# The narrow experts of a mixture-of-experts layer: plain float32 products in two column halves in place of split float32r products

## What is computed

```python
def swiglu(x, w_gate, w_up, w_down):
    return (jax.nn.silu(x @ w_gate) * (x @ w_up)) @ w_down

def moe_swiglu(x, router_w, router_b, w_gate, w_up, w_down):
    ...
    top_logit, top_e = lax.top_k(logits, TOP_K)
    gate = jax.nn.softmax(top_logit, axis=-1)
    ...
    # rows of a token are handed to its two experts, and come back times their gates
    y_rows = lax.map(block, (rows_tok.reshape(n_blk, MOE_BLOCK), blk_e)).reshape(n_rows, d)
    y_rows = y_rows * rows_g[:, None]
    out = jnp.zeros((t + 1, d), x.dtype).at[rows_tok].add(y_rows)[:t]
```

## Time and profile before

| | us |
|---|---|
| median of 3 runs | 1460.13 |
| lowest and highest run | 1458.97, 1460.23 |
| the profiled execution | 1458.71 |
| its span, from the first to the last instruction | 1456.9 |
| PE busy in the span | 1411.5 |
| DVE busy in the span | 1195.6 |
| ACT busy in the span | 981.3 |

### The profile page before, as it was taken

How to read it: one execution, slowest core, us unless ns; L and a number is a source line. 1 busy time by engine, 2 the same in 40 slices (tenths; PEclk the granted TensorE clock), 3 DMA queues, 4 the chain that set the end, 5 groups by cost and what they waited for, 6 DMA issues and landing times.

```text
span 1456.9 us, 18432 instructions
## 1 busy us (share of the span) xinstructions
PE 1411.5 (97%) x6906; PEld 1148.9 (79%) x6906; DVE 1195.6 (82%) x1232; ACT 981.3 (67%) x991; POOL 55.4 (4%) x95
## 2 busy tenths in 40 slices
PE   9999999999999999999989998999989999989967
PEld 7898888888888988888878776777767777767855
DVE  6787977654546778887699998999989999989967
ACT  6347634644345337653578888899979998979855
POOL 2000000000000000000210000000000000000010
PEclk9999999999999999999999999999999999999989
DMA  8544555455555644554879999999999999999980
GB/s 332 208 159 167 188 181 190 158 203 200 175 199 178 213 169 158 191 181 174 326 301 392 420 422 389 410 421 422 421 407 417 422 420 420 422 395 407 421 337 31
DMA packets 79360, 424.16 MB, mean 291 GB/s; under 512 B 9185, under 2 KB 9361, under 8 KB 45473
## 3 DMA queue, kind: packets, MB, share of 16 engines
q1 hardware_dynamic: 72864, 402.16, 70.8%
q0 software_dynamic: 5984, 20.15, 4.1%
q10 hardware_dynamic: 416, 0.60, 0.1%
HBM read 414.48 MB, written 8.39 MB: 290 GB/s over the span
## 4 chain that ended last, share of the span: by engine, by line
PE 85%; DVE 6%; issue 3%; ACT 3%; DMA 2%; SPq 0%; POOL 0%; DVEq 0%; ACTq 0%; POOLq 0%
PE ps L886 21%; PE ps L1424 14%; PE ps L1419 9%; PE ps L1185 8%; PE ps L1440 7%; PE ps L863 5%; PE ps L874 5%; PE ps L1435 4%; PE ps L1162 4%; DVE w_lo L2134 2%; ACT w_hi L1621 1%; DVE w_lo_x L2134 1%; DMA late<-dense_dram 1%; PE ps L1369 1%; ACT w_hi_x L1621 1%
## 5 line engine op out<-in xcount | busy, mean ns | idle before, releaser
L1995 DVE TENSOR_TENSOR w_lo<-raw_m,w_hi 128x2048 fp32r<-128x2048 f32 x113 | 257.7, 2289 | 110.9 <-ACT w_hi L1548 110.9
L1548 ACT CAST w_hi<-raw_m 128x2048 fp32r<-128x2048 f32 x113 | 214.6, 1907 | 125.8 <-PE ps L886 56.0
L2134 DVE TENSOR_TENSOR w_lo<-late,w_hi 128x2048 fp32r<-128x2048 f32 x99 | 224.9, 2282 | 9.7 <-ACT w_hi L1621 9.2
L2134 DVE TENSOR_TENSOR w_lo<-raw_m,w_hi 128x2048 fp32r<-128x2048 f32 x99 | 224.0, 2283 | 7.5 <-ACT w_hi L1621 7.0
L1621 ACT CAST w_hi<-late 128x2048 fp32r<-128x2048 f32 x99 | 188.7, 1910 | 19.1 <-PE ps L1440 9.7
L1621 ACT CAST w_hi<-raw_m 128x2048 fp32r<-128x2048 f32 x99 | 187.9, 1910 | 17.9 <-PE ps L1440 5.9
L886 PE MATMUL ps<-w_hi,hT_hi 128*128 128x512 f32 x464 | 183.2, 395 | 0.2 <-DVE w_lo L1995 0.2
L886 PE MATMUL ps<-w_hi,hT_lo 128*128 128x512 f32 x464 | 180.9, 390 | 0.0
L886 PE MATMUL ps<-w_lo,hT_hi 128*128 128x512 f32 x464 | 180.7, 389 | 0.0
L2134 DVE TENSOR_TENSOR w_lo_x<-late,w_hi_x 128x2048 fp32r<-128x2048 f32 x66 | 150.6, 2282 | 5.0 <-ACT w_hi_x L1621 4.6
L1621 ACT CAST w_hi_x<-late 128x2048 fp32r<-128x2048 f32 x66 | 126.2, 1912 | 12.1 <-PE ps L1440 6.2
(11 more groups left out here) (444 smaller groups left out, 2801.6 us busy)
## 6 DMA issues: line engine op xcount, KB each, us to landing
late<-experts_dram SPq DMA_DIRECT2D x165, 1024.0 KB, 10.0
raw_m<-dense_dram SPq DMA_DIRECT2D x226, 512.0 KB, 4.3
raw_m<-experts_dram SPq DMA_DIRECT2D x99, 1024.0 KB, 10.1
bias<-b_in_dram POOLq DMA_DIRECT2D x26, 256.0 KB, 5.9
late<-dense_dram SPq DMA_DIRECT2D x4, 512.0 KB, 10.3
raw_m<-front_dram SPq DMA_DIRECT2D x4, 384.0 KB, 4.5
raw_m<-front_dram SPq DMA_DIRECT2D x2, 768.0 KB, 7.7
x_rows<-prow POOLq DMA_DIRECT2D x3, 512.0 KB, 12.6
```

The lines of the kernel that those rows point to most:

```text
L1548: copy(w_hi[:, g % RS, :], slot_raw(g, False)).then_inc(hi_ready, 1)
L1995: tt(w_lo[:, g % RS, :], slot_raw(g, False), w_hi[:, g % RS, :], ALU.subtract)\
L2134: tt(lo_slot(m), slot_raw(m, True), hi_slot(m), ALU.subtract).then_inc(lo_ready, 1)
```

## The change

Chunks of light slots are no longer split. PE takes them from the raw slot after the landing (semaphore moe_in), as plain float32. The 64 rows are the 64 columns of a half of the array; one half of the output columns goes to partitions 0 to 63 of the result, the other to 64 to 127 of the same bank. For "gu" that is four blocks by two halves of 256 columns (each half takes 128 gate and 128 up columns), for "dn" two blocks by two halves of 512. Hence no low half, no sum, no split of the hidden rows, one transpose of 128 x 128, and rows that POOL stores in two parts of 64 x 512. The raw slot of a light chunk is free when PE has used it (light_used, or the bank's semaphore), and the ring of split slots counts heavy chunks alone (ORDINAL). LEAD, TAIL and BETWEEN have other values, so light and heavy steps alternate otherwise. The gathered rows are added at slice 10 of the last expert and after its last "dn" chunk's products are issued.

```diff
-    LEAD, TAIL = 6, 7
-    BETWEEN = ((0, 1, 3, 4, 6, 7, 9, 10),) * 3 + ((0, 2, 4, 6, 7, 9, 10),)
+    LEAD, TAIL = 5, 5
+    BETWEEN = ((0, 1, 2, 3, 5, 6, 7, 9, 10), (0, 2, 3, 5, 6, 7, 9, 10)) * 2
...
-            SUM_AT[m + 2] = s, i
-            LT_AT[m + 5] = s, i
-        ROWSUM_AT[AT[s, "dn", NF - 1, 0] + 2] = s
...
+    HEAVY_CHUNKS = [m for m, key in enumerate(MS0) if key[0] in HEAVY]
+    ORDINAL = {m: j for j, m in enumerate(HEAVY_CHUNKS)}
+    NH = len(HEAVY_CHUNKS)
...
-        low_rows = over("low_rows", [P, W], ytok_at + 4 * MIX)
-        down_rows = over("down_rows", [P, P], bias_at + 4 * 1024)
+        light_x = nc.alloc_sbuf_tensor_at("light_x", [P, KT, T], f32, offset=hT_hi_at)[:, :, P:P + LC]
+        light_y = nc.alloc_sbuf_tensor_at("light_y", [P, KT, T], f32, offset=hT_lo_at)[:, :, P:2 * P]
...
+        def split_turn(pas, m):
+
+            return MOE_BASE + (NH + m if pas else ORDINAL[m])
+
         def slot_free(pas, m):
 
-            n = MOE_BASE + pas * NM + m
-            if pas or m >= RX:
+            n = split_turn(pas, m)
+            if pas or n - MOE_BASE >= RX:
                 return last_use(n - RX)
             return last_use(n - RS) if m < RS else (merged_ready, L * NT)
+
+        def raw_free(pas, m):
+
+            prev, of = (m - RE, pas) if m >= RE else (NM + m - RE, 0)
+            if of or prev not in LIGHT_USED:
+                return lo_ready, split_turn(of, prev) + 1
+            kind, v = LIGHT_USED[prev]
+            if kind == "raw":
+                return light_used, v
+            b, k = FILL[v]
+            return full[b], k + 1
...
-                        sp.wait_ge(lo_ready, MOE_BASE + pas * NM + m - RE + 1)
+                        sp.wait_ge(*raw_free(pas, m))
...
-                if m in ROWSUM_AT:
+                if (kind, i) == ("dn", NF - 1) and s in LIGHT:
+                    b, k = FILL[(0, s), "acc", 0]
+                    pool.wait_ge(drained[b], k + 1)
                     for h in range(2):
-                        b, k = FILL[(0, ROWSUM_AT[m]), "rowsum", h]
-                        pool.wait_ge(drained[b], k + 1)
-                    at_row = Y_BASE[ROWSUM_AT[m]]
-                    pool.dma_start(y_rows[at_row:at_row + LC, :], yl_rows).then_inc(y_out_l, 16)
+                        pool.dma_start(y_rows[Y_BASE[s]:Y_BASE[s] + LC, h * W:(h + 1) * W], yl_rows[h * LC:(h + 1) * LC, :])\
+                            .then_inc(y_out_l, 16)
...
-                    await_drained((0, s), f"sum{i}")
+                    await_drained((0, s), f"gu{i}")
                     b = claim((0, s), f"hT{i}")
-                    for k in range(2):
-                        ins = nc.tensor.transpose(ps[:, b, k * LC:(k + 1) * LC], hid_l[:, k * P:(k + 1) * P],
-                                                  ident[0:LC, 0:LC])
-                    done(ins, (0, s), f"hT{i}")
+                    done(nc.tensor.transpose(ps[:, b, 0:P], hid_l, ident[:, :]), (0, s), f"hT{i}")
...
-                if m in ROWSUM_AT:
-                    s = ROWSUM_AT[m]
-                    for h in range(2):
-                        b = claim((0, s), "rowsum", h)
-                        done(mm(ps[:, b, :], down_rows[LC:P, :], ysb_lo[LC:P, 4 * h:4 * h + 4, :], start=False, stop=True,
-                                skip_group_check=True), (0, s), "rowsum", h)
-                if m in SUM_AT:
-                    s, i = SUM_AT[m]
-                    b = claim((0, s), f"sum{i}")
-                    done(mm(ps[:, b, :], down_rows[LC:P, :], low_rows[LC:P, :], start=False, stop=True,
-                            skip_group_check=True), (0, s), f"sum{i}")
...
+            def light_chunk(l, m, kind, i, c, w):
+
+                s = l[1]
+                if kind == "gu":
+                    b = claim(l, f"gu{i}") if c == 0 else FILL[l, f"gu{i}", 0][0]
+                    for kk in range(4):
+                        k = 4 * c + kk
+                        if kk == 2:
+                            between(m)
+                        both = w[:, kk * W:(kk + 1) * W].rearrange("p (a q n) -> p a q n", a=2, q=2)
+                        for q in range(2):
+                            ins = mm(ps[q * LC:(q + 1) * LC, b, 0:2 * P].rearrange("p (a n) -> p a n", a=2),
+                                     light_x[:, k, :], both[:, :, q, :], start=(k == 0), stop=(k == KT - 1),
+                                     skip_group_check=True)
+                    if c:
+                        done(ins, l, f"gu{i}")
+                    return ins
+                b = claim(l, "acc") if i == 0 else FILL[l, "acc", 0][0]
+                for kk in range(2):
+                    if kk:
+                        between(m)
+                    for h in range(2):
+                        ins = mm(ps[h * LC:(h + 1) * LC, b, :], y_light(s, i)[:, kk * LC:(kk + 1) * LC],
+                                 w[:, kk * D + h * W:kk * D + (h + 1) * W], start=(i == 0 and kk == 0),
+                                 stop=(i == NF - 1 and kk == 1), skip_group_check=True)
+                if i == NF - 1:
+                    done(ins, l, "acc")
+                return ins
+
             def streams():
                 first_gather()
-                pe.wait_ge(down_ready, 2)
...
-                    pe.wait_ge(lo_ready, MOE_BASE + m + 1)
-                    w = hi_slot(m), lo_slot(m)
+                    if s in LIGHT:
+                        pe.wait_ge(moe_in[m % RE], 16 * (m // RE + 1))
+                        ins = light_chunk(l, m, kind, i, c, slot_raw(m, True))
+                        if LIGHT_USED[m][0] == "raw":
+                            ins.then_inc(light_used, 1)
+                        continue
+                    j = ORDINAL[m]
+                    pe.wait_ge(lo_ready, MOE_BASE + j + 1)
+                    w = hi_slot(j), lo_slot(j)
...
-                            if s in LIGHT:
-                                for r in range(2):
-                                    ins = mm(ps[:, b, :], hT_hi[:, k, P:2 * P], w[r][:, kk * W:(kk + 1) * W],
-                                             start=(k == 0 and r == 0), stop=(k == KT - 1 and r == 1),
-                                             skip_group_check=True)
-                            else:
-                                for pa, (a, r) in enumerate(for_3):
...
-                    if m + 3 < NM:
+                    if m + 3 in ORDINAL:
...
-                        copy(y_light(*last_l)[0], ps[:, b, 0:2 * LC].rearrange("p (m n) -> p m n", m=2)).then_inc(hi_part, 1)
+                        copy(y_light(*last_l), ps[:, b, 0:P]).then_inc(drained[b], 1)
...
-                        copy(low_rows[LC:P, :], ps[LC:P, b, :]).then_inc(drained[b], 1)
+                        if last_l:
+                            await_full((0, last_l[0]), f"hT{last_l[1]}")
+                        A(hid_l, ps[:, b, 0:P], ACT.Silu).then_inc(silu_ready, 1)
...
-                        for h in range(2):
-                            b = await_full(l, "acc", h)
-                            copy(ysb_lo[LC:P, 4 * h:4 * h + 4, :], ps[LC:P, b, :].rearrange("p (m n) -> p m n", m=4))\
-                                .then_inc(drained[b], 1)
+                        b = await_full(l, "acc")
+                        copy(yl_rows, ps[:, b, :]).then_inc(drained[b], 1)
...
-                        await_gain()
-                        for k in range(KT):
-                            ins = stt(hT_hi[:, k, P + LC:2 * P], ps[:, b, k * LC:(k + 1) * LC], gain(k),
-                                      hT_hi[:, k, P:P + LC], ALU.mult, ALU.subtract)
-                        ins.then_inc(drained[b], 1)
-                    if m in SUM_AT:
-                        g, n = SUM_AT[m]
-                        b = await_full((0, g), f"sum{n}")
-                        nsl += 1
-                        dve.wait_ge(silu_ready, nsl)
-                        tt(hid_l, hid_l, ps[0:LC, b, 2 * P:4 * P], ALU.mult).then_inc(drained[b], 1)
-                    if (kind, c) == ("gu", 1) and s in HEAVY:
+                        tt(light_x, ps[:, b, :].rearrange("p (k n) -> p k n", k=KT),
+                           cols[:, L - 1, C_FG:C_FG + KT].unsqueeze(2).to_broadcast([P, KT, LC]), ALU.mult)\
+                            .then_inc(drained[b], 1)
...
-                    if (s, kind, c) == (E - 1, "gu", 0) and i in (6, 7, 8, 10):
-                        add_picked((6, 7, 8, 10).index(i))
+                    if (s, kind, i) == (E - 1, "gu", NF - 1):
+                        add_picked(c)
...
                     if (s, kind, i) == (E - 1, "dn", NF - 1):
+                        add_picked(2)
+                        add_picked(3)
```

More of the change, by code:

```diff
@@ L270, in program @@
                     USED.append(("w", n_used))
+    LIGHT_USED, n_light = {}, 0
     for pas in range(2):
-        for e, kind, i, c in (MS0, MS1)[pas]:
+        for m, (e, kind, i, c) in enumerate((MS0, MS1)[pas]):
+            light = pas == 0 and e in LIGHT
```

(30 more changed lines are left out.)

86 lines of the change are left out of this document (32 added, 54 removed).

## The result

The changed kernel takes 1436.99 us (median of 4 runs, 1436.54 to 1437.85) against 1459.55 for the kernel before (1458.96 to 1460.23): a ratio of 0.9846, with a 95% interval of 0.9829 to 0.9863. That is 22.6 us less, 2.0 us above the forecast of 1435, and inside the range. The profiled run has a span of 1436.0 us.

The account below looks back on a forecast made before the run. Transfers were taken as the bound: last landing 1420.5 - 6.8 - 3.3 = 1410.4, plus 11 behind it, plus tail 12.2, less 0.6 at the start, a span of 1433; with 1.8 outside, 1435 us. Range 1418 to 1451 (8 in 10).

Parts of the forecast that it names:

- The floor after: Whole expert stage after the change: transfers still end last, last landing 1410.4 us, last expert product 1421.4.
- The floor before: Expert stage of the kernel before: transfers at 421 GB/s, 14.94 us per six chunks, taken as the floor that stays.
- dips of 6.5 and 6.8 us: Transfer time lost at 880 to 910 plus 1290 to 1320 us (6.5), and at 1390 to 1420 us (6.8).
- PE alone: Whole stage if PE set the end: last product at 1395 to 1415 us, or 1415 to 1435 with 6.65 us light steps.
- rival 1: Every light step: column halves overlap less than for the heads, PE becomes the bound and the kernel slower; chance 0.10.
- The end: Last expert: gathered-row adds moved to slice 10 and past it, so the whole 6.8 us lost at 1390 to 1420 goes.
- T + 17: Due time of the first gathered-row add, T being the last light product's end; rows ready near T + 15.5, margin 1.5 us.
- rival 2: End of the last expert: gathers late again, last hidden product waits for DVE, 1443 to 1450 us; chance 0.10.
- Start: First expert product at 739.3 us: PE no longer waits for down_rows, 0 to 1 us gained, 0.6 taken.
- Held slots: Light chunks' raw slots, held until PE has used them: costs 0 to 3 us in all.
- Splits worth nothing in the steady stretch: Light chunks' dropped casts and subtractions (252 us ACT, 301 us DVE) give nothing there, only slack where the flow breaks.
- Rivals 3, 4 and 5: 3: held slots thin transfers, 1475, 0.03; 4: does nothing, 1457 to 1462, 0.04; 5: splits were floor, 1409 to 1429, 0.05.

## Why the prediction was right, and where it was not

*The floor after: right.* The sum by transfers put the last landing at 1410.4 and the last expert product at 1421.4; they came at 1411.9 and 1422.7. The rate was the one forecast, and the time is 2.0 us off. That the kernel would come to stand on its transfers is what the halved loads showed.

*The floor before: wrong.* The step "I take the transfers as the floor that stays" reads a DMA share of 1.01 as the cause. Halved loads left the kernel before at 1459.2. Six chunks in PE's 15.04 us are 6.29 MB / 15.04 us = 418 GB/s, so PE's pace and the transfers' limit differ by less than 1%, and a queue that always has the next load in it looks full at either. The chain had said it: from one step to the next it went through PE alone. The sum had a sign of it as well: the last expert product ended 24.3 us behind the last landing, where the prediction's own terms make 13.6 (split 4.2, last down product 2.7, backlog 6.7). So it was not the transfers lost in the dips of 6.5 and 6.8 us that held the kernel up, but PE's stands in the same places; with halved loads they are just as long (busy 44.56 of 50 us from 850 to 900, 44.52 with whole loads). That the sum held all the same is luck: PE's pace in the kernel before happened to lie within 1% of the transfers' limit, so a time worked out from the old landing was also one for the new floor. With a slower PE before, the same steps would have put the time too high.

*PE alone: too high.* The forecast was 1409 to 1429 us with the tail, the run with halved loads gave 1394. One term was the light step. A pair takes 1015.70 - 1001.32 = 14.38 us, so the light step is 14.38 - 8.43 = 5.95, not 6.2 to 6.65; a unit of 256 columns is 1.72 / 4 = 0.43 us, as the whole-array rows had it, and entering the light form costs 0.15 us (1.01 - 0.86, and 2.74 - 2.58), leaving it 0.2 (4.32 - 4.12). That is 11 us in 44 steps. The other term was the remainder, taken as 12 to 32 us: the last expert product of the run with halved loads is

```profile
1375.26 4.11 PE ps L1474 x18
```

and 1379.4 - 739.3 - 44 x 14.38 leaves 7.4. (The pair of 256 columns that the prediction puts at 0.437 us is 0.433 by its rows; nothing hangs on it.) So "transfers still end last, narrowly" should have been by 43 us; it did not matter for the time, only for rival 1.

*Rival 1 (halves overlap less)* falls: 5.33 / 2.74 = 1.95 and 3.43 / 1.72 = 1.99 of 2. The figure that the Trainium skill gives in "TensorE: Matmul & The Clock Gate", section "Measured speedup vs the span model", 2.38 for three column tiles, 0.79 of the ideal, is not what two halves show here.

*The end: right in kind, wrong in due times.* The 6.8 us hole went, and the adds' place alone is 12 to 13 us. But the adds were not due near T + 17: T is 1392.98, the first add ran at 1416.45, T + 23.5, with no wait. The one that came late is the fourth, since its rows reuse the first's. That is rival 2 in small: 1.1 us in the tail, 13.3 for 12.2.

*Start: wrong in sign, though small.* It was put at 0.6 us gained. PE's first product no longer waits for down_rows, but PE then stands 6.0 us, to 749.3, for the first hidden rows (DVE's product of gate and up, line 2657). Behind that stand the granted clock is 0.50, the lower level of 1.2 GHz, until about 754, and 15 products take 5.44 us in place of 3.44. The changed kernel, and below it the kernel before at the same place:

```profile
749.00:754.00 5.00, 4.71 (x12) 3.79 (x13) 4.39 (x11) 2.27 (x2) 3.93 (x3) 0.50 0.78 223
...
749.98 5.44 PE ps L1462 x15
...
750.03 3.44 PE ps L1424 x15
```

So PE is 2.0 us later there than before.

*Held slots:* put at 0 to 3 us. In the steady stretch they cost nothing, but while PE is late after the start the loads wait for light slots that PE still holds: 229 and 357 GB/s at 780 to 790 and 800 to 810 us, 4.6 + 1.5 = 6.1 us of transfer. The kernel before lost 2.2 us nearby (376 and 375 GB/s from 770 to 780 and 790 to 800). A shorter LEAD did not help, and what the hole costs in the end stays open.

*Splits worth nothing in the steady stretch:* right for the changed kernel (1439.6 with DVE loaded again). In the kernel before, halving the light subtractions alone gave 7.8 us.

*Rivals 3, 4 and 5* fall by the time and by the rate, 419 GB/s with light slots held and DVE half idle.

The account of 22.6 us is then: PE's need falls by 65, and the transfers, which were level with PE, give 43 of it back. What the 65 are made of can be read from the kernel before, to its last expert product, beside the run with halved loads shown above:

```profile
740.00:1445.00 705.00, 675.40 (x2926) 525.32 (x2924) 659.44 (x541) 590.94 (x563) 20.50 (x22) 0.98 0.96 392
```

PE's stands fall from 29.6 to 6.0 us. The largest that go are the 11.3 behind the gathers and 14.4 where a heavy expert changes (two kinds are shown with the halved subtractions; a third is 0.7). PE's busy time falls by 42. The light steps are about 27 of that, with 0.66 us in 34 pairs and some 0.5 in ten single ones. The other 15 I did not take apart. A part may be the granted clock, whose mean was 0.988 over the span before and 0.996 with halved loads; behind the stands it was low, as here from 1080 to 1090 us in the kernel before:

```profile
1080.00:1090.00 10.00, 7.84 (x27) 6.45 (x28) 5.43 (x8) 5.21 (x8) 0.56 (x1) 0.66 1.01 417
```

## What to carry to other kernels

When two resources run at the same pace, neither a full share nor a steady rate says which one sets it; a run with half of one's work does, and the chain of waits is the better guess until then. Work out the need of each resource alone over the whole stage: the time after a change is the larger of them (here 1437 by transfers; 1394 by PE, and 1451 and 1621 once PE was loaded), and what a change saves beyond the next one is lost. A step that waits for a long round trip belongs behind the work that feeds others on its engine: this alone was half of the gain, and needed none of the new arithmetic.

## What the hardware showed that was not expected

Row gathers landed after very different times: 4.3 to 9.4 us with a median of 7.6 in the changed kernel, 4.1, 5.2 and 8.0 (least, median, most) in the kernel before, 4.2 to 6.0 in the changed kernel with halved loads, and up to 12.0 in the kernel before with the adds moved. That more chunks in flight make them slower would fit some of these and is not shown. They don't share a queue with the chunks, as the prediction's rival 2 had it: from 1390 to 1425 us of the changed kernel the profile has the chunks on q1 and the 2.36 MB of stores and gathers on q0. One issue on POOL took between 0.95 and 2.75 us, in either kernel; the changed one and, below it, the one before:

```profile
1404.62 2.51 POOL L815 DMA_INDIRECT late<-y_rows,bias  x1 [0.30 <-issue]
1407.44 0.95 POOL L815 DMA_INDIRECT prow<-y_rows,bias  x1 [0.30 <-issue]
...
1405.09 2.75 POOL L792 DMA_INDIRECT late<-y_rows,bias  x1 [2.16 <-DVE xt L2520]
```

Two plain float32 products in the two column halves, on the same bank of results, cost PE what one of them costs on the whole array, 0.43 us for 256 columns.
